# First w_in slab in two transfers, bias tables asked for later, one adaLN row moved, first expert read in place

## The reference, cut to what matters

```python
def first_block(x, c, w_ada, ..., w_in, ..., rel_bias, w_out, w_router, ..., w_up, b_up, w_down, b_down):
    mod = jnp.dot(jax.nn.silu(c), w_ada[l]) + b_ada[l]           # 6 x 1024 numbers
    sh1, sc1, gt1, sh2, sc2, gt2 = [m[:, None, :] for m in jnp.split(mod, 6, axis=-1)]
    h = rmsnorm(x, g_pre_mix[l]) * (1.0 + sc1) + sh1
    z = jnp.dot(h, w_in[l])                                      # 1024 x 3360
    ...                                # z split into q_m k_m v_m o_m i_m f_m q_a kc vc ks vs kw vw g_a
    y_m = mlstm(...) * jax.nn.sigmoid(o_m)                       # 4 heads of 128
    y_a = nsa(..., rel_bias)                                     # 8 heads of 64, relative biases on the logits
    y = jnp.dot(jnp.concatenate([y_m, y_a], axis=-1), w_out[l])
    x = x + gt1 * rmsnorm(y, g_post_mix[l])
    h2 = rmsnorm(x, g_pre_ffn[l]) * (1.0 + sc2) + sh2
    y2 = moe(h2, ...)                  # 32 experts, the best 4 of each token, clamped SwiGLU, 1024 wide
    x = x + gt2 * rmsnorm(y2, g_post_ffn[l])
# second_block: its own adaLN vector, one wide projection w_in_2, indexed sparse attention
# beside a state-space branch, gated merge, output projection, residual
```

## Time and profile before

| | us |
|---|---|
| runs, median | 1806.37 |
| runs, lowest and highest | 1804.97, 1807.29 |
| the profiled execution | 1804.96 |
| its span | 1803.2 |
| PE busy | 1717.5 (95%) |
| DVE, ACT, POOL busy | 546.1, 416.0, 110.3 |

### The profile page before, as it was taken

One profiled execution on the slowest core, in us unless ns is written; L12 is line 12 of the kernel. 1 busy time (PEld: TensorE's weight loads), 2 busy tenths in 40 slices (PEclk: granted clock), 3 DMA queues, 4 the chain that ended last, 5 costly groups with the idle time before them and its releaser, 6 DMA issues. The chain is left out here.

```text
span 1803.2 us, 39637 instructions
## 1 busy us (share of the span) xinstructions
PE 1717.5 (95%) x17283; PEld 998.8 (55%) x17283; DVE 546.1 (30%) x761; ACT 416.0 (23%) x704; POOL 110.3 (6%) x121
## 2 busy tenths in 40 slices
PE   5999988999999999999999999999986999999998
PEld 3875653334344343443443434434335988899898
DVE  2264153111111111111111111111134656577664
ACT  2244143100000000000000000000004358645452
POOL 0111020000000000000000000000000034401000
PEclk9999999999999999999999999999997999999999
DMA  9986395999999999999999999999961634344372
GB/s 348 342 284 236 141 339 209 360 393 404 392 396 400 401 405 393 399 398 404 388 405 392 401 401 395 403 396 399 385 222 42 195 117 137 121 141 133 102 206 75
DMA packets 187878, 545.45 MB, mean 302 GB/s; under 512 B 16216, under 2 KB 90216, under 8 KB 154952
## 3 DMA queue, kind: packets, MB, share of 16 engines
q1 hardware_dynamic: 172432, 519.49, 76.3%
q10 hardware_dynamic: 10968, 15.40, 2.4%
q0 software_dynamic: 4416, 9.69, 1.6%
HBM read 526.06 MB, written 17.84 MB: 302 GB/s over the span
## 5 line engine op out<-in xcount | busy, mean ns | idle before, releaser
L1430 PE MATMUL ps<-ring_low,xg 128*32 128x512 f32 x3072 | 343.8, 596 | 0.0
L1430 PE MATMUL ps<-first_ring,xg 128*32 128x512 f32 x3072 | 335.4, 592 | 0.0
L1561 DVE TENSOR_SCALAR gl<-ps 128x768 f32<-128x768 f32 x32 | 30.6, 957 | 683.3 <-PE ps L1430 683.3
L1430 PEld LDWEIGHTS ps<-first_ring,xg 128*32 128x32 f32 x3072 | 99.5, 110 | 230.1 <-issue 230.1
L1430 PEld LDWEIGHTS ps<-ring_low,xg 128*32 128x32 f32 x3072 | 96.5, 110 | 205.8 <-issue 199.9
L1453 PE MATMUL ps<-first_ring,aT 128*32 128x256 f32 x3072 | 173.3, 382 | 2.3 <-ACT aT L1512 2.3
L1453 PE MATMUL ps<-raw_more,aT 128*32 128x256 f32 x3072 | 171.6, 379 | 0.0
L1453 PEld LDWEIGHTS ps<-first_ring,aT 128*32 128x32 f32 x3072 | 100.4, 111 | 82.6 <-issue 20.3
L1506 ACT ACTIVATE sg<-gl 128x768 f32<-128x768 f32 x32 | 27.0, 844 | 511.6 <-DVE gl L1561 511.6
L1453 PEld LDWEIGHTS ps<-raw_more,aT 128*32 128x32 f32 x3072 | 99.8, 110 | 65.9
L1511 ACT ACTIVATE aT<-ps 128x576 f32<-128x576 f32 x32 | 20.8, 650 | 443.9 <-PE ps L1441 434.1
(11 more groups left out here) (500 smaller groups left out, 1875.0 us busy)
## 6 DMA issues: line engine op xcount, KB each, us to landing
first_ring<-in_w_up_dram SPq DMA_DIRECT2D x128, 1024.0 KB, 6.8
ring_low<-in_w_up_dram SPq DMA_DIRECT2D x128, 1024.0 KB, 6.9
raw_more<-in_w_down_dram SPq DMA_DIRECT2D x64, 1024.0 KB, 7.3
first_ring<-in_w_down_dram SPq DMA_DIRECT2D x64, 1024.0 KB, 6.9
ring_low<-in_w_in_dram SPq DMA_DIRECT2D x39, 1024.0 KB, 5.3
first_ring<-in_w_ada_dram SPq DMA_DIRECT2D x7, 2048.0 KB, 20.4
ring_low<-in_w_ada_dram SPq DMA_DIRECT2D x5, 2048.0 KB, 17.2
y_dram<-ye ACTq DMA_DIRECT2D x32, 288.0 KB, 5.8
```

The lines of the kernel that those rows point to most:

```text
L1430: mm = pe.matmul(ps[32 * q:32 * q + 32, u, :], xg[:, k, 32 * block_of:32 * block_of + 32], w[:, :, 256 * f:256 * f + 256], start=False, st ...
L1561: dve.tensor_scalar(gl[:], ps[:, 0:3, 0:256], LIMIT, None, ALU.min).then_inc(s(tag, "glu_ready"), 1)
```

## The change: what it does

- **USE1.** ("in", "v") and ("mod", 9) change places: v becomes slab 14, row 9 becomes slab 15.
- **Slab qa.** It is loaded by two DMAs of 256 columns (1 MB, 1 KB pieces). The first signals first_half, the second slab_ready of slot 4. half(0) waits for first_half, half(1) for slab_ready.
- **Tables.** ACT's wait for rv_stored and its two table DMAs move from ahead of first_row_copy(2) to behind the 8 shift additions.
- **Row 9.** PE runs half(11) ahead of mod(9); ACT does take(11) ahead of mod_row_copy of row 9.
- **First expert.** up for expert 0 reads its rows from xsel directly and its selection column from sel3 by a broadcast, and waits for no xg_ready. ACT does rows of expert 1 first, then sigmoid of expert 0, and no rows of expert 0. In the rare second pass over the experts ("more_") nothing changes.

```diff
--- before.py
+++ after.py
@@ -128,7 +128,7 @@
 
 USE1 = [("mod", m) for m in range(4)]
 USE1 += [("in", "qa"), ("in", "kv"), ("in", "tok"), ("mod", 4), ("mod", 5), ("in", "q"), ("mod", 6), ("mod", 7), ("in", "k"),
-         ("mod", 8), ("mod", 9), ("in", "v"), ("mod", 10), ("mod", 11), ("in", "o")]
+         ("mod", 8), ("in", "v"), ("mod", 9), ("mod", 10), ("mod", 11), ("in", "o")]
 USE1 += [("out", 0), ("mod", 12), ("out", 1), ("mod", 13), ("mod", 14), ("mod", 15), ("mod", 16), ("mod", 17)]
 N_OF = {use: n for n, use in enumerate(USE1)}
 
@@ -455,7 +455,14 @@
             def _(sp):
                 sp.dma_start(xtok, A["x"].rearrange("(t p) d -> p t d", p=P)).then_inc(sm("x_in"), 16)
                 for n in range(N_OF["in", "o"] + 1 + SLOTS):
-                    load_slab(sp, n, SLABS1[n])
+                    if n == N_OF["in", "qa"]:
+
+                        for h, sem in enumerate((sm("first_half"), sm(f"slab_ready{n % len(slots)}"))):
+                            at = Z_QA + 256 * h
+                            sp.dma_start(slots[n % len(slots)][:, :, 256 * h:256 * h + 256],
+                                         A["w_in"][:, at:at + 256].rearrange("(k p) n -> p k n", p=P)).then_inc(sem, 16)
+                    else:
+                        load_slab(sp, n, SLABS1[n])
 
             @block.gpsimd
             def _(pool):
@@ -505,15 +512,15 @@
                 first_row_copy(0)
                 first_row_copy(1)
                 norm_root(act, 1)
-                act.wait_ge(sm("rv_stored"), 16)
-                for par in range(2):
-                    src = bass.AP(rv_dram.tensor, rv_dram.offset + par * RV, [[1, P], [2 * RV, AH // 2], [1, SEQ]])
-                    act.dma_start(tbr[:, par * 4:par * 4 + 4, :], src).then_inc(sm("tb_in"), 16)
                 first_row_copy(2)
                 first_row_copy(3)
                 for k in range(KT):
                     act.wait_ge(sm("h_scaled"), k + 1)
                     act.activation(hT[:, k, :], hT[:, k, :], ACT.Identity, bias=mod[:, k:k + 1]).then_inc(sm("h_ready"), 1)
+                act.wait_ge(sm("rv_stored"), 16)
+                for par in range(2):
+                    src = bass.AP(rv_dram.tensor, rv_dram.offset + par * RV, [[1, P], [2 * RV, AH // 2], [1, SEQ]])
+                    act.dma_start(tbr[:, par * 4:par * 4 + 4, :], src).then_inc(sm("tb_in"), 16)
 
                 def take(i):
                     name, h = HALVES1[i]
@@ -609,8 +616,8 @@
                 take(10)
                 mod_row_copy(act, N_OF["mod", 8], 8, 4, 2)
                 turned(2, 0, 4)
+                take(11)
                 mod_row_copy(act, N_OF["mod", 9], 9, 4, 2)
-                take(11)
                 turned(3, 0, 2)
                 mod_row_copy(act, N_OF["mod", 10], 10, 4, 2)
                 take(12)
@@ -627,7 +634,9 @@
                 def half(i):
                     name, h = HALVES1[i]
                     n = N_OF["in", name]
-                    if h == 0:
+                    if i == 0:
+                        pe.wait_ge(sm("first_half"), 16)
+                    elif h == 0 or i == 1:
                         pe.wait_ge(sm(f"slab_ready{n % len(slots)}"), slab_count(SLABS1, n))
                     if i >= 2:
                         pe.wait_ge(sm("in_taken"), i - 1)
@@ -783,8 +792,8 @@
                 pe.wait_ge(sm("scores_taken"), 4)
                 pe.wait_ge(sm("c_copied"), 1)
                 turn(2, 0, 4)
+                half(11)
                 mod(9)
-                half(11)
 
                 pe.wait_ge(sm("qk_ready"), 2)
                 pe.wait_ge(sm("pt_ready"), ROUND_AT[3])
@@ -1416,18 +1425,21 @@
 
             @block.tensor
             def _(pe):
-                def up(tag, n, between=lambda: None):
-                    pe.wait_ge(s(tag, "xg_ready"), n * 2 + 2)
+                def up(tag, n, between=lambda: None, rows_at=None, one_at=None):
+
+                    rows_at, one_at = (rows_at, one_at) if rows_at is not None else (xg, one3[:])
+                    if rows_at is xg:
+                        pe.wait_ge(s(tag, "xg_ready"), n * 2 + (0 if tag == "" else 2))
                     for u in range(3):
                         for q, _, _, f in TILES[u]:
                             cols_of = bup[:].rearrange("b (c n) -> b c n", c=2)[:, :, 256 * f:256 * f + 256]
-                            pe.matmul(ps[32 * q:32 * q + 32, u, :], one3[:], cols_of, start=True, stop=False)
+                            pe.matmul(ps[32 * q:32 * q + 32, u, :], one_at, cols_of, start=True, stop=False)
                     for k in range(UPS):
                         pe.wait_ge(s(tag, f"raw_in{k}"), n * 16 + 16)
                         w = raw[k].rearrange("p (c n) -> p c n", c=2)
                         for u in range(3):
                             for q, _, block_of, f in TILES[u]:
-                                mm = pe.matmul(ps[32 * q:32 * q + 32, u, :], xg[:, k, 32 * block_of:32 * block_of + 32],
+                                mm = pe.matmul(ps[32 * q:32 * q + 32, u, :], rows_at[:, k, 32 * block_of:32 * block_of + 32],
                                                w[:, :, 256 * f:256 * f + 256], start=False, stop=(k == UPS - 1))
                         mm.then_inc(s(tag, "up_used"), 1)
                         if k == 1:
@@ -1463,7 +1475,7 @@
                                            start=True, stop=True)
                     mm.then_inc(s(tag, "bias_summed"), 1)
 
-                up("", 0)
+                up("", 0, rows_at=xsel, one_at=sel3[:, 0:1].to_broadcast([3 * NE, 32]))
                 with pe.Fori(0, NE - 1) as i:
                     pe.wait_ge(s("", "glu_ready"), i + 1)
                     pe.wait_ge(s("", "lin_ready"), i + 1)
@@ -1521,9 +1533,8 @@
                     act.dma_start(y_dram[bass.ds(row, ROWS), 768:D].rearrange("(u p) n -> p u n", u=3), ye[ROWS:P])\
                         .then_inc(s(tag, "ye_stored"), 16)
 
-                rows("", 0, 0)
+                rows("", 1, 0)
                 sigmoid("", 0)
-                rows("", 1, 0)
                 with act.Fori(0, NE - 1) as i:
                     turned("", i)
                     sigmoid("", i + 1)
```

## The result

The changed kernel takes 1794.7 us (median of 6 runs, 1791.54 to 1798.49), the kernel before 1805.51 in the same series: a ratio of 0.9941, 95% interval 0.9927 to 0.9956. The profiled execution takes 1795.37 us with a span of 1793.6, 9.6 us less than the span before. The forecast was 1796.4 and 10.0 us less. The total is right; two of its terms are not.

The account below looks back on a forecast made before the run. PE bounds the kernel (95% busy, expert loop a fixed block), so only its earlier idle and slow time can be gained: 2.6 + 5.0 + 1.6 + 0.8 = 10.0 us, from median 1806.37 to 1796.4, range 1792.0 to 1801.0.

Parts of the forecast that it names:

- slab qa and tables: At half(0): with qa split and tables later, PE starts 2.9 us earlier; term 2.6 us, bounds 1.2 and 3.0.
- row 9: Behind turn(2, 0, 4): half(11) ahead of mod(9) saves 3.5 us idleness and 1.5 slow clock; 5.0 us, bounds 3.5 and 5.2.
- first expert: Waits for xg go: 1.6 us at expert 0 and 0.8 us at expert 1; no clock gain counted.
- the slab is what PE waits for: Before half(0): slab qa, issued at 16.71, lands at 39.5 and ends PE's 4.45 us of idleness.
- the first tile of hT is there at about 36.65: Before half(0): ACT's shift additions begin at 36.21, so PE can start at 36.65, 2.9 us earlier.
- The landing itself: Slab qa's first half lands at 33.7 to 34.5, 34.8 at worst, before the first tile of hT.
- Rival (a): At half(0): PE starts at 36.65 but stays slow until 43.0, leaving 1.2 to 1.5 of 2.6 us; 1797.6 us, chance 0.16.
- rival (b): Before the experts: the clock holds after the shorter idle stretch, adding 2.5 us; 1793.9 us, chance 0.09.
- Here it fell at 288.9, about when PE will start: At expert 0: argument that the clock falls despite the shorter idle stretch, against a further 2.5 us gain.
- The idle stretch: Ahead of expert 0: PE's idle time falls from 5.33 to about 3.7 us.
- Rival (d): At flip: tables land late behind a full queue and PE waits; 1808.4 us, or 1810.1 with fallen clock; chance 0.04.
- 7 us of cover: Before flip: tables asked for at 39.5 land by 52; flip needs them at 61.90 less 2.9.

Follow-up runs that it names:

- the pair above: Two profiled kernels, ratios against the kernel before: the whole change, run again, 0.9933; the whole change but for the first expert edit, 0.9963.

## Why the prediction was right or wrong

The parts, each as the gain of its own kernel and by the traces:

| part | forecast | alone, by ratio (interval) | in the traces |
|---|---|---|---|
| slab qa and tables | 2.6 | 0.2 (-1.4 to 1.8) | 0 to 2.7 at half(0) |
| row 9 | 5.0 | 4.0 (2.3 to 5.6) | 5.35, 5.4 |
| first expert | 2.4 | 3.4 (1.8 to 5.1) | 2.4; 5.2 and 5.8 with the clock |

**Slab and tables: wrong.** The step that failed is the pair "the slab is what PE waits for" and "the first tile of hT is there at about 36.65". Both were true of one execution. In five profiles of kernels without these edits the first addition starts at 36.21, 36.26, 36.41, 37.65 and 39.86, and half(0) starts 3.35, 3.11, 2.42, 0.93 and 0.66 us later. Less the 0.65 us that remains with the edits, that is 2.7, 2.5, 1.8, 0.3 and 0.0, a mean of 1.4 us. The timed kernels put it at 0.2 to 0.5 us alone (up to 2.2 by the widest interval), and at -0.4 and 1.1 us between the whole change and the one without it. The landing itself was forecast well: 34.8 us at worst for the first half, 34.4 to 35.5 measured with both edits. Rival (a) gave about the right size, with a wrong reason but for one profile: the gap itself was smaller, and the clock took something back only in the first profile after.

**Row 9: right,** in idleness, clock and next release; the trace gives 5.35 us.

**First expert: the waits right, the clock wrong.** The forecast gave its clock no gain and called it rival (b) at 9 in 100. It is the usual case: no fall in 4 of the 6 profiles that have the edit and its idle stretch. The clock at expert 1 stood nowhere in the forecast, and the pair above has 1.7 us there. "Here it fell at 288.9, about when PE will start" took the moment of one execution for a property of the program. The idle stretch also came out shorter (3.26 us) than the 3.7 of the forecast.

So the total was right in part by luck: an overrated term and an underrated one met. The parts do not seem to add: row 9 and the expert alone give 7.4 us together, the kernel with both 11.0 (8.7 to 13.2). The difference is 3.6 us, give or take 3.2 if the three intervals are independent. A cause is at hand, though not shown: the clock holds at expert 0 in 4 of the 5 profiles that have both of these edits and the idle stretch, and fell in the only profile with the expert edit alone; and in 4 of the 7 without the expert edit, that of row 9 alone among them, 1.7 us are lost again at expert 1. More profiles of the expert edit alone would settle whether its gain of clock needs row 9's shift.

**Rival (d)** did not happen, but the margin I called 7 us of cover was near a cliff: 6 us later the same transfer took 29 us.

## What to carry to other kernels

When PE waits for the later of two things, the gain of hurrying one is the gap between them, and a single profile gives one draw of it: look at the gap in several executions before pricing it. Price an idle stretch with its slow clock behind it, and do so for the shortened stretch too; here the clock was about half of what the expert edit gave beside the others. Where parts draw on the clock, time them together as well as alone: what one gives can depend on the others. A transfer moved later in a full queue should be judged by what is issued just behind its new place, not by the cover counted from its old duration.

## What the runs showed of the hardware

- The granted clock of the windows table reads 1.00 until its first change in the trace. At the start that is not PE's speed: 16 records of 128x128 took 3.62 us at 14.76 in the kernel before and 1.91 us at 14.34 with ten matmuls ahead of them.
- The same program had its slow stretches at other places in two executions: from 20.6 to 24.0 and 37.7 to 41.1 in one profile of the changed kernel, from 37.0 to 43.8 in the other, by the granted clock before 190 us. The Trainium skill (TensorE: Matmul & The Clock Gate, What's actually happening) says that the clock's moments run freely of the kernel; the two traces agree.
- At the start of expert 1 a wait of 2.8 us was followed by a fall of the clock in 4 of 7 profiles, one of 2.1 us in 1 of 7. At expert 0 it was 7 of 7 with waits of about 5 us, and 2 of 6 with the shorter ones. Those two waits were 3.56 and 3.59 us, the four without a fall 3.3 us; whether the wait or the clock is the cause of that difference stays open.
